# Order of the ring places of the expert matrices, and the products of constants before the first expert

## The reference

```python
def run_block(args):
    e, toks, w = args
    xb = x_pad[toks]
    h = jax.nn.silu(xb @ w_gate[e]) * (xb @ w_up[e])
    return (h @ w_down[e]) * w[:, None].astype(xb.dtype)
```

## Time and profile before

| | us |
|---|---|
| median of 3 runs | 1726.93 |
| lowest, highest | 1723.77, 1729.46 |
| the profiled execution | 1724.58 |
| its span, first to last instruction | 1722.8 |
| TensorE busy in the span | 1651.0 (96%) |
| VectorE, ScalarE, GpSimd busy | 661.5, 339.5, 163.3 |
| read from HBM | 307.90 MB |

### The profile page before, as it was taken

How to read it: one execution, slowest core, us unless ns; L and a number is a source line. 1 busy time by engine, 2 the same in 40 slices (tenths; PEclk the granted TensorE clock), 3 DMA queues, 4 the chain that set the end, 5 groups by cost and what they waited for, 6 DMA issues and landing times.

```text
span 1722.8 us, 22549 instructions
## 1 busy us (share of the span) xinstructions
PE 1651.0 (96%) x9299; PEld 1015.7 (59%) x9300; DVE 661.5 (38%) x1395; ACT 339.5 (20%) x670; POOL 163.3 (9%) x169
## 2 busy tenths in 40 slices
PE   8999999999999999999999999999999999999990
PEld 5556777777776666666688555654444444444340
DVE  1446454545542323232577644541112221211125
ACT  1112232223231222212112000011111111111115
POOL 1000000000003321121000000001111111111110
PEclk9999999999999999999899999899999999999995
DMA  7200121211017544342352533388999999999975
GB/s 230 59 21 20 50 62 50 59 53 50 24 63 209 190 160 153 123 147 99 118 207 97 210 134 135 124 295 330 395 391 382 383 409 388 388 385 384 387 276 201
DMA packets 104410, 337.67 MB, mean 196 GB/s; under 512 B 24378, under 2 KB 68482, under 8 KB 87924
## 3 DMA queue, kind: packets, MB, share of 16 engines
q1 hardware_dynamic: 89572, 276.22, 42.6%
q0 software_dynamic: 13568, 55.78, 10.7%
q10 hardware_dynamic: 1168, 4.23, 0.6%
HBM read 307.90 MB, written 35.51 MB: 199 GB/s over the span
## 4 chain that ended last, share of the span: by engine, by line
PE 87%; DMA 8%; DVE 2%; issue 1%; ACT 1%; SPq 0%; POOL 0%; DVEq 0%; POOLq 0%; ACTq 0%
PE psum L1070 12%; PE psum L1184 10%; PE psum L1510 6%; PE psum L1515 6%; DMA arena<-in_w_up 6%; PE psum L1372 6%; PE psum L1387 5%; PE psum L1536 4%; PE psum L1111 4%; PE psum L1223 3%; PE psum L974 3%; PE psum L1542 3%; PE psum L1084 2%; PE psum L1523 2%; PE psum L1129 2%; PE psum L1118 2%
## 5 line engine op out<-in xcount | busy, mean ns | idle before, releaser
L1070 PE MATMUL psum<-arena 128*128 128x258 f32 x896 | 215.3, 384 | 0.0
L1184 PE MATMUL psum<-arena 128*128 128x344 f32 x576 | 182.3, 458 | 0.0
L1070 PEld LDWEIGHTS psum<-arena 128*128 128x128 f32 x896 | 162.8, 190 | 27.9 <-issue 7.0
L1516 PE MATMUL psum<-arena 128*64 128x512 f32 x320 | 141.6, 595 | 0.0
L1515 PE MATMUL psum<-arena 128*64 128x512 f32 x320 | 141.6, 595 | 0.0
L1510 PE MATMUL psum<-arena 128*128 128x512 f32 x320 | 139.8, 595 | 1.1 <-DVE arena L2547 1.1
L1184 PEld LDWEIGHTS psum<-arena 128*128 128x128 f32 x576 | 103.2, 190 | 53.0 <-issue 11.2
L1510 PEld LDWEIGHTS psum<-arena 128*128 128x128 f32 x320 | 60.0, 190 | 73.4 <-issue 73.0
L1372 PE MATMUL psum<-arena 128*128 128x258 f32 x448 | 100.5, 389 | 0.9 <-ACT arena L1797 0.9
L1387 PE MATMUL psum<-arena 128*128 128x512 f32 x224 | 99.2, 595 | 0.0
L1372 PEld LDWEIGHTS psum<-arena 128*128 128x128 f32 x448 | 87.0, 194 | 14.5 <-issue 1.3
(11 more groups left out here) (394 smaller groups left out, 2138.5 us busy)
## 6 DMA issues: line engine op xcount, KB each, us to landing
arena<-in_w_gate SPq DMA_DIRECT2D x32, 2048.0 KB, 22.1
arena<-in_w_up SPq DMA_DIRECT2D x32, 2048.0 KB, 27.2
arena<-in_w_down SPq DMA_DIRECT2D x32, 2048.0 KB, 39.5
arena<-in_w_in SPq DMA_DIRECT2D x33, 512.0 KB, 5.1
gates<-arena SPq DMA_DIRECT2D x16, 516.0 KB
arena<-gates SPq DMA_DIRECT2D x16, 516.0 KB, 6.2
arena<-in_x_prompt SPq DMA_DIRECT2D x16, 512.0 KB, 4.7
arena<-in_w_o SPq DMA_DIRECT2D x1, 4096.0 KB, 16.8
```

The lines of the kernel that those rows point to most:

```text
L1070: ins = mm(psum[:, BANK[name[0]], 0:QT], held, moved, start=(k == 0 and name in ("X1", "V6", "Y5")), stop=(k == 3), skip_group_check=True)
L1184: ins = mm(psum[:, FB + t, 0:SP3], wring[:, u, k, :], xT[:, k, t * SP3:(t + 1) * SP3], start=(k == 0), stop=(k == KD - 1))
L1516: u = mm(psum[64:P, 3, :], xgT[:, xpar, k, 0:64], wu[:, k, :], start=(k == 0), stop=(k == KD - 1))
```

## The change

Three edits. `place(j)`, `earlier(j)` and `AGAIN` are replaced by a table that is worked out: `MULTIPLIED` is the order in which TensorE uses the matrices (g0, u0, g1, u1, d0, ...), and from j = 12 on matrix j takes the place of the matrix that is used as number j - 10 in that order. u3 and d3 take the two late places, 8 and 9, as before. `ln2g` and `ln2b` lie in place 6, not 9, and SyncE waits for the last matrix of that place (g29) where it waited for d29. And `keep_busy` is called with 0 for 10 ahead of the first expert.

```diff
--- before.py
+++ after.py
@@ -254,7 +254,7 @@
         row_f2, blk_f = z(2, NT), z(2, NT)
 
         fin = at(Z0, NT, D)
-        ln2g, ln2b = at(ring_at[9], D), at(ring_at[9] + D, D)
+        ln2g, ln2b = at(ring_at[6], D), at(ring_at[6] + D, D)
 
         z = Zone(Z4, END)
         ident = z(P)
@@ -508,7 +508,6 @@
             return P if full(n) else P // 2
 
         RING = len(ring_at)
-        AGAIN = (0, 1, 8, 9, 2, 3, 4, 5, 6, 7)
         FIRST = 1 << 16
         assert T * NE < FIRST
 
@@ -530,18 +529,23 @@
         def rest_at(n):
             return P // 2 if three(n) else 0
 
+        MULTIPLIED = [0, 1] + [m for n in range(1, NE) for m in (3 * n, 3 * n + 1, 3 * n - 1)]
+        before, place_of, turn_of = [], [], []
+        for j in range(3 * NE):
+            b = MULTIPLIED[j - 8] if j in (8, 9) else MULTIPLIED[j - RING] if j > 11 else None
+            before.append(b)
+            place_of.append(place_of[b] if b is not None else j - 2 if j > 9 else j)
+            turn_of.append(turn_of[b] + 1 if b is not None else 0)
+
         def place(j):
-            return j if j < 8 else AGAIN[(j - 8) % RING]
-
-        def earlier(j):
-            return [i for i in range(j) if place(i) == place(j)]
+            return place_of[j]
 
         def ring(j):
             v = at(ring_at[place(j)], MAT)
             return v.rearrange("p (k n) -> p k n", n=D if j % 3 == 2 else FE)
 
         def landed(j):
-            return WE_BASE[place(j)] + 16 * (len(earlier(j)) + 1)
+            return WE_BASE[place(j)] + 16 * (turn_of[j] + 1)
 
         w_in = a["w_in"][0].rearrange("(k p) n -> p k n", p=P)
 
@@ -753,8 +757,8 @@
 
             def load_matrix(j, e):
 
-                if earlier(j):
-                    n, m = divmod(earlier(j)[-1], 3)
+                if before[j] is not None:
+                    n, m = divmod(before[j], 3)
                     sp.wait_ge((g_done, u_done, d_done)[m], n + 1)
                 elif place(j) >= 8:
                     sp.wait_ge(ws_dve, 1)
@@ -784,7 +788,8 @@
                 e = expert_at(n)
                 for m in range(3):
                     load_matrix(3 * n + m, e)
-            sp.wait_ge(d_done, NE - 2)
+            n, m = divmod(max(j for j in range(3 * NE) if place(j) == 6), 3)
+            sp.wait_ge((g_done, u_done, d_done)[m], n + 1)
             sp.dma_start(ln2g, a["ln2_g"][0].partition_broadcast(P)).then_inc(ln1_ld, 16)
             sp.dma_start(ln2b, a["ln2_b"][0].partition_broadcast(P)).then_inc(ln1_ld, 16)
             with sp.If(sp.value_load(ov_on[0:1, 0:1].bitcast(I32), min_val=0, max_val=1)):
@@ -1498,7 +1503,7 @@
             pe.wait_ge(sel_dve, MORE)
             pe.wait_ge(blk_dve, 1)
             mm(psum[:, 2, 0:NE + 1], more_w[0:NE], tri[0:NE, 0:NE + 1], start=True, stop=True).then_inc(pos_done, 1)
-            keep_busy(10, 1)
+            keep_busy(0, 1)
 
             def turn_block(par, rows=P):
                 for k in range(KD):
```

## The result

| | us |
|---|---|
| kernel before, median of 4 runs | 1727.72 (1723.77 to 1729.46) |
| changed kernel, median of 4 runs | 1715.37 (1713.13 to 1716.52) |
| ratio, with its 95% interval | 0.9928 (0.9909 to 0.9947) |
| profiled execution, before and after | 1724.58, 1713.13 |
| its span, before and after | 1722.8, 1711.4 |

The span is 11.4 us shorter. The lines of the changed code stand four or five further down: L1399 is `keep_busy`, L1510 the turns, L1515 the first projections, L1528 the projections of 32 tokens, L1541 a down projection, L765 SyncE's issues, L908 the scatters.

A forecast was written before the change was run, and what follows sets the result against it. The load stream was taken as the bound, slightly slower than TensorE. Gains of 5.3 (part 1) and 6.6 (part 2) make 11.9 us: 1712.7 from the profiled execution, 1715.0 from the median; forecast 1714, range 1704 to 1721.

The forecast's parts named there:

- The turns: TensorE's eight turns of the gathered rows, before the first expert: start at about 1116.6 and not 1124.48, 7.9 us earlier.
- The clock: TensorE's clock, low into the first up projection once the constants go: costs 1.7 us after 1119.6 (0 to 3.5).
- g4: Load of expert 4's gate matrix: waits for an earlier-used place, so it is issued at 1148.1 and not about 1168.
- u4: Load of expert 4's up matrix: lands at 1171.0 and not 1182.9, so the load stream gains 11.9 us.
- The pace: Load stream in the steady expert loop: one matrix lands every 5.99 us, as before the change.
- rival C: Steady part, 1180 to 1660 us: more open loads slow the stream's pace; at 6.22 us a matrix, about 1732; chance 0.04.
- B: Rival: only the front gains; the head start is lost at 6.07 us a matrix, or the clock stays low: 1720; chance 0.16.
- The end: Last scatters, after the expert loop: they follow the last matrix's landing and end 12 us earlier.
- The waits: TensorE's waits for up matrices in the expert loop: fall from 8.8 us to 2 or 3.
- part 1: Ahead of the first expert: ten products of constants go, moving TensorE 5.3 us earlier (3.5 to 7.0).
- part 2: SyncE's load ring: places given out in the order of use close the hole at 1158 to 1169, gaining 6.6 us.
- Rival A: Expert loop: TensorE's own work, not the load stream, sets the end; 16.6 us go: 1708, or 1702 to 1708; chance 0.20.

The follow-up runs named there:

- the parts alone: Two kernels, each the kernel before with one part: without the ten products of constants, 1721.27 us; with the new order of ring places, 1719.35 us.
- e2: The changed kernel with the ten products of constants put back, so only the new order of ring places remains: 1719.35 us, ratio 0.9952 to the kernel before.
- e3: The changed kernel without the load of one up matrix, that of the 17th expert: 1711.33 us.
- e5: The changed kernel without the loads of three up matrices (n = 6, 11 and 16): 1711.39 us.
- e6: The changed kernel with the scatters of the first 26 experts cut to 16 rows each: 1710.34 us.
- e8: The changed kernel run again, unaltered: 1713.78 us, ratio 0.9928 to the kernel before.
- e10: The changed kernel run a third time, unaltered: 1716.15 us.

## Why the prediction was right

**The time.** Forecast 1714, range 1704 to 1721; measured 1715.4. The mechanism was the one forecast: the load stream gains a head start by two holes that close, and the end follows the stream. Against the profile, step by step:

- *The turns* were to start at 1116.6 and start at 1116.65. *The first projection* was to start at 1119.6; it is 1119.76. *The clock* was to cost 1.7 us after that; the first projections take 15.37 for 13.97 us, which is 1.4. TensorE is 5.4 us ahead, the sum said 5.3.
- *g4* was to be issued at 1148.1 and is at 1148.23. *u4* was to land at 1171.0 and lands at 1170.1: the head start is 12.8 us for 11.9. The 0.9 us come from d3, which was to land at 1159.0 and lands at 1158.0: its load takes 16.3 us, and the sum had the 17.1 of before.
- *The pace* was taken as unchanged, 5.99 us. That term was off by a little: in six profiles with the new order it is 6.01 to 6.02, in three with the old 5.99 to 6.00. The means are 6.014 and 5.990; over 82 matrices the 0.025 us between them make 2.0 us that are lost again, 2.4 in the pair of before and after. It may be rival C's mechanism (more loads open at once) or B's, at a sixth of the size from which C decides (0.025 for 0.15 us); no run separates the two. d31 lands 10.4 us earlier, not 11.9.
- *The end* was to be 12 us earlier and is 11.4 for the last scatter as for the span. The chain still starts where the stream ends.
- *The waits* were to fall to 2 or 3 us and are 2.6.
- *The profiled execution* was to take 1712.7 us and took 1713.13. That it came so near is in part luck: d3's 0.9 us and the pace's 2.4 have opposite signs, and the executions of one kernel lie 3 to 13 us apart.

**Both parts were sized about right.** In medians the parts alone give 6.0 (said 5.3) and 7.9 (said 6.6), with both forecasts inside the intervals. Before against after, counted from the last dense product, part 1 is 48.2 - 42.5 = 5.7 us up to expert 1 and part 2 576.4 - 570.3 = 6.1 behind it. In the first table the new order moves u4, relative to TensorE, by 12.8 - 5.4 = 7.4 us in the changed kernel and by 3.9 + 4.0 = 7.9 in e2; the pace takes some 2 of it back.

**Rival A had the amount but not the time.** TensorE was said to be able to move 16.6 us. The three terms hold: in e3, e5 and e6 it wins 11.6 us inside the loop (from expert 1's projections to its last product, against before), where 8.8 + 2.5 = 11.3 were said, and 5.4 at the start in the changed kernel's profile, 17.0 together. In the changed kernel and its two repeats it wins 7.4 to 7.8 in the loop, so the stream keeps 3.8 to 4.2 us from it; e3 sets just these free. But A's 1708 takes both together, and the runs of e3, e5 and e6 end at 1710 to 1711: in their profiles the long stretch of low clock leaves 1.7 us of the start at best. Without the stretch's 5.3 us they would come out at some 1705 to 1706, inside A's 1702 to 1708; that is an estimate which takes their other runs to have had the stretch too, and no run shows it. The stretch is the one thing that the prediction did not foresee. Its argument on the clock covered only what comes after 1116, with three bounds from short stretches; that the clock could be low from 1100 on was outside them. It does not touch the gain of part 1, since the constants cost 5.5 us with it and 5.6 without. The two profiles of before are both short; that the kernel before can be long too is only made likely, by the spread of its runs and their clocks.

**What stays open.** Why the pace rises by 0.025 us with the new order, what decides between the short and the long stretch, and why loads of 120 partitions are so dear. No version that does the whole work beat the changed kernel.

## What to carry to other kernels

When two resources are nearly level, look for the holes in the slower one before the steady part: a late place in a ring that is given out in another order than that of use makes a queue idle once, at the start, and the whole stream is late by that from then on. Count such a gain only up to the slack of the second resource, here some 4 us inside the loop, and measure that slack by taking one load away and then three: where the second step gives hardly more, the second resource has taken over. Count in such profiles from a common point, and look at the clock behind it: here one stretch of low clock was worth 5.3 us, as much as each part of the change. Products that keep a clock up are worth it only as long as what they wait for isn't there yet; these ran 8 us past it.

## What the runs showed of the hardware

- The granted clock around 1100 to 1130 us, under small and spaced products of the router, was at 1.2 GHz for 3.4 and 6.8 to 10.2 us (five profiles), or for 23.9 to 27.3 us in one stretch (nine), and one and the same program showed both (e8, e10). The Trainium skill, "TensorE: Matmul & The Clock Gate", section "What's actually happening", says of a kernel's first products that the number of slow ones varies from run to run; these traces show the like in mid-kernel, and the difference here is 13.7 us of low clock (27.3 against 3.4 + 10.2) and 5.3 us on the way to expert 1. The same section of the Trainium skill holds the cost at the start to be under 1% of a typical span; here it is 0.3%.
- Ten loads of 2 MB, cut into 120 and 8 partitions, brought the whole stream from 387 to 298 GB/s (1400 to 1640 us) with the engines' share still at 1.00: the share says that engines are occupied, not that they move what they could.
- The scatters' bytes cost the load stream time although both have their own queues: with 16 rows a scatter the pace is 5.67 us a matrix for 6.01. By then the queue is short (d31 lands 10.3 us after its issue, for 35.1), so that TensorE's releases rather than the engines seem to set it.
